# Throwaway matmuls ahead of and between the chain steps of the gated delta section (two-layer hybrid decoder step, one core)

## The reference

```python
def gdn_mixer(h, ...):
    z = h @ w_in                                  # q, k, v, beta, g, gate
    q, k, v = silu(conv(...)), l2-normalized q and k
    o, S = gated_delta_chunked(q, k, v, g, beta, S0)      # chunks of 64 tokens
    return (o * rsqrt(mean(o * o)) * norm_g * silu(zg)) @ w_out

def gated_delta_chunked(...):
    T = inverse(I + A)                            # per chunk, unit triangular
    u, w = T @ (v * beta), T @ (kb * exp(gc))
    def step(S, inp):                             # 4 steps for the sequence of 256
        v_new = u_c - w_c @ S
        o = qg_c @ S + qk_c @ v_new
        S = gl_c * S + kd_c.T @ v_new
        return S, o
```

## Time and profile before

| | |
|---|---|
| median of 3 runs | 1581.13 us (1579.74 to 1581.99) |
| the profiled execution | 1569.06 us, span 1566.9 us |
| mean granted TensorE clock in it | 0.956 |
| PE busy | 1434.2 us (92%) |
| DVE busy | 823.6 us (53%) |
| ACT busy | 628.2 us (40%) |
| POOL busy | 377.8 us (24%) |

### The profile page before, as it was taken

How to read it: one execution, slowest core, us unless ns; L and a number is a source line. 1 busy time by engine, 2 the same in 40 slices (tenths; PEclk the granted TensorE clock), 3 DMA queues, 4 the chain that set the end, 5 groups by cost and what they waited for, 6 DMA issues and landing times.

```text
span 1566.9 us, 30542 instructions
## 1 busy us (share of the span) xinstructions
PE 1434.2 (92%) x12048; PEld 1355.4 (86%) x12048; DVE 823.6 (53%) x1075; ACT 628.2 (40%) x955; POOL 377.8 (24%) x352
## 2 busy tenths in 40 slices
PE   7999999676898799999999999989987778999997
PEld 7999989576588589999989999979876748999996
DVE  4444456974373364444454444478757456544444
ACT  4333346531042353333353333365574234533333
POOL 3333002532131123331113331100017442233200
PEclk9999999898599899999999999999989798999999
DMA  7455532200052145555425555424323014355551
GB/s 279 162 162 185 167 120 95 96 3 33 36 183 79 40 155 162 164 168 186 151 93 163 161 173 183 142 75 148 122 89 123 28 68 148 121 162 166 184 166 49
DMA packets 50616, 203.29 MB, mean 130 GB/s; under 512 B 5697, under 2 KB 5697, under 8 KB 49761
## 3 DMA queue, kind: packets, MB, share of 16 engines
q1 hardware_dynamic: 46224, 181.03, 35.0%
q0 software_dynamic: 4016, 19.81, 3.5%
q10 hardware_dynamic: 288, 1.18, 0.2%
HBM read 192.17 MB, written 9.83 MB: 129 GB/s over the span
## 4 chain that ended last, share of the span: by engine, by line
PE 79%; DVE 11%; ACT 5%; issue 4%; POOL 0%; DMA 0%; DVEq 0%; ACTq 0%; POOLq 0%
PE gemm L2321 21%; PE gemm L2325 21%; PE gemm L2322 21%; DVE wlo L2284 2%; PE gemm L2341 2%; PE job L2354 2%; ACT whi L2279 2%; PE job L689 1%; DVE M L1905 1%; DVE M L2071 1%; PE job L1583 1%; PE job L812 0%; PE job L1657 0%; PE job L720 0%; PE job L1546 0%
## 5 line engine op out<-in xcount | busy, mean ns | idle before, releaser
L2284 DVE TENSOR_TENSOR wlo<-raw,whi 128x1024 fp32r<-128x1024 f32 (+1 forms) x319 | 426.4, 1337 | 461.9 <-ACT whi L2279 461.8
L2321 PE MATMUL gemm<-xhi,whi 128*128 128x288 f32 x2040 | 619.4, 304 | 32.2 <-DVE wlo L2284 22.3
L2325 PE MATMUL gemm<-xlo,whi 128*128 128x288 f32 x2040 | 607.3, 298 | 4.6 <-DVE xlo L395 4.4
L2322 PE MATMUL gemm<-xhi,wlo 128*128 128x288 f32 x2040 | 608.7, 298 | 0.0
L2279 ACT ACTIVATE whi<-raw 128x1024 fp32r<-128x1024 f32 (+1 forms) x319 | 358.1, 1123 | 493.5 <-PE gemm L2325 490.0
L2321 PEld LDWEIGHTS gemm<-xhi,whi 128*128 128x128 f32 x2040 | 389.5, 191 | 43.8 <-DVE wlo L2284 26.0
L2325 PEld LDWEIGHTS gemm<-xlo,whi 128*128 128x128 f32 x2040 | 390.7, 191 | 5.8 <-DVE xlo L395 5.1
L2322 PEld LDWEIGHTS gemm<-xhi,wlo 128*128 128x128 f32 x2040 | 389.9, 191 | 1.4
L2321 PE MATMUL gemm<-hhi,whi 128*128 128x288 f32 x704 | 208.8, 297 | 0.9 <-DVE wlo L2284 0.9
L2322 PE MATMUL gemm<-hhi,wlo 128*128 128x288 f32 x704 | 207.7, 295 | 0.0
L2325 PE MATMUL gemm<-hlo,whi 128*128 128x288 f32 x704 | 207.0, 294 | 0.0
(11 more groups left out here) (381 smaller groups left out, 1299.1 us busy)
## 6 DMA issues: line engine op xcount, KB each, us to landing
raw<-in_w_dram SPq DMA_DIRECT2D x255, 512.0 KB, 3.5
raw<-in_w_dram SPq DMA_DIRECT2D x64, 704.0 KB, 4.0
M<-in_ret_in_dram POOLq DMA_DIRECT2D x1, 2048.0 KB, 9.5
out_ret_s_dram<-M POOLq DMA_DIRECT2D x1, 2048.0 KB, 8.0
s_space<-in_gdn_in_dram POOLq DMA_DIRECT2D x4, 512.0 KB, 7.9
M<-in_gdn_in_dram POOLq DMA_DIRECT2D x4, 512.0 KB, 6.0
out_gdn_s_dram<-s_space POOLq DMA_DIRECT2D x4, 512.0 KB, 4.7
out_gdn_s_dram<-M POOLq DMA_DIRECT2D x4, 512.0 KB, 4.2
```

The lines of the kernel that those rows point to most:

```text
L2284: nc.vector.tensor_tensor(wlo[c % SPL][:, 0:w], raw[c % RAW][:, 0:w], whi[c % SPL][:, 0:w].bitcast(F32), ALU.subtract).then_inc(lo_ready, 1)
L2321: pe.matmul(bank[:, 0:T], whi[s][:, w], hi[:, f0 + q, :], start=first, stop=False)
L2322: pe.matmul(bank[:, 0:T], wlo[s][:, w], hi[:, f0 + q, :], start=False, stop=False)
L2325: mm = pe.matmul(bank[:, 0:T], whi[s][:, w], lo[:, f0 + q, :], start=False, stop=last)
```

## The change

A helper `keep_busy(n)` issues n matmuls on PE whose results nobody reads: `mean` (128 x 128) by the first 256 columns of `xsum`, float32, into `gemm[0]`. Ahead of the chain PE waits until `gemm[0]` was read out for the last time before `gdo`, and issues six. In the chain there are two after each `dKS` (steps 1 to 3), two after `dU` of step 0, two after `dO` of steps 0 to 2, and two after `updates` of steps 1 and 2. With the six that makes 24.

```diff
+            def keep_busy(n):
+                for _ in range(n):
+                    pe.matmul(gemm[0][:, 0:SEQ], C("mean"), xsum[:, 0:SEQ], start=True, stop=True)
+
+            wait_count(pe, bank_free[0], TABLE["gdo"][3][0])
+            keep_busy(6)
             for ck in range(4):
...
                     fin(mm, ("dKS", ck))
+                    keep_busy(2)
...
                 for e in range(2):
                     fin(mms[e], ("dU", ck, e))
+                keep_busy(2 if ck == 0 else 0)
                 if ck == 0:
                     to_channels(0)
...
                 if ck < 3:
                     outputs()
+                    keep_busy(2)
                 if ck in (1, 2):
                     updates(0, ck - 1)
+                    keep_busy(2)
                     if ck == 2:
                         state_products(1)
                     head_norms(ck - 1)
```

## The result

| | before | after |
|---|---|---|
| median | 1581.56 us (4 runs, 1579.74 to 1583.48) | 1562.58 us (4 runs, 1561.32 to 1563.83) |
| ratio | | 0.9894, interval 0.9855 to 0.9932 |
| profiled execution | 1569.06 us, span 1566.9 | 1563.83 us, span 1561.7 |
| PE busy | 1434.2 us | 1443.3 us |

The change saves 19 us by the medians and 5 us by the two profiled executions. The forecast was 7 us, and its range reached down to 1570 us only. In a second comparison the changed kernel again had 1563.5 us and the kernel before 1578.5 us.

The account below looks back on a forecast made before the run. PE, or something it waits for, was taken to bound nearly everywhere, with 24 us at the low clock in the chain. Gains of 7.7 us less 0.3 for overruns, taken as 7.3, gave 1574.0 us, range 1570.0 to 1580.

Parts of the forecast that it names:

- The step that failed: Whole kernel: the profiled execution's gain of 7.3 us applies unchanged to the median, 1581.1 to 1573.8 us, forecast as 1574.0.
- The first rival: Chain: the low-clock stretch is missing in some executions, which then run 1 us slower; median 1578.5 us, chance 0.22.
- `dU` to `dKV` in step 0: Start of the chain: 3.10 us falls to about 2.8, a gain of 0.3, with the pair itself costing 0.6.
- `dKV` to `dKS`: Second term, step 0 into step 1: 4.66 us falls to 3.23, a gain of 1.4, ACT being late next.
- `dKS` to `dU`: Third term, in step 1: 2.86 us falls to 2.6, a gain of 0.3, DVE being late next.
- the overruns: Steps 1 to 3: pairs longer than their pauses cost 0.3 us in all, bounds 0 and 1.2 us.
- The lower bound: Sum of the chain's gains: at worst DVE and ACT hide another 1.4 us and overruns are 1.2, leaving 5.1 us.
- the signs: Profile after: clock 1.00 from 1230 to 1290 us, step 2's `dU` near 1253 instead of 1260.8, `gdo` near 1288.
- The price of the fillers: Matmuls of 256 columns: a pair takes 0.87 us and six 2.6 at the high clock, 1.74 and 5.2 at the low.
- The slower rival: Chain: fillers don't hold the clock, and pairs at 1.74 us on the path add 4.7 us, 1585.8 us; chance 0.09.
- What comes behind: After the chain, `gdo` only shifts; its low-clock loss of 2.7 us may vary by 1.5 us either way.
- The rule on short pauses between groups: Chain: by this rule the clock falls again between groups despite fillers; gain 5.9 us instead of 7.3, 1575.2 us, chance 0.07.

Follow-up runs that it names:

- 2: The kernel before against itself, no edit, with a second profile: 1576.95 us, ratio 0.999 (0.9962 to 1.0017).
- 11: The kernel before, no edit, a single profiled execution: 1578.93 us.
- 12: The kernel before, no edit, another single profiled execution: 1583.48 us.
- narrow control 5: The changed kernel without pairs, its six matmuls ahead of the chain cut from 256 to 16 columns: 1576.6 us, ratio 1.0008 against the kernel before.
- three wide, 6: The changed kernel without pairs and with three matmuls of 256 columns ahead of the chain instead of six: 1569.92 us, ratio 0.9968 against the kernel before.
- pairs alone, 4: The changed kernel without the six matmuls ahead of the chain, pairs kept: 1567.69 us, ratio 0.9935 against the kernel before.
- six alone, 3: The changed kernel without all pairs, the six matmuls ahead of the chain kept: 1563.09 us, ratio 0.9909 against the kernel before.
- after, 1: The changed kernel again, no edit, on one chip with the kernel before: 1563.51 us, ratio 0.9909 (0.9883 to 0.9936).
- lean, 7: The changed kernel without the pairs after `dKS` and after `dU` of step 0: 1561.64 us, ratio 0.9922 against the kernel before.
- experiment 9: The changed kernel without pairs after `dKS` and step 0's `dU`, plus fillers behind the chain and at one place of the first layer's mixer: 1563.22 us, ratio 0.9931.

## Why the prediction was wrong

**The step that failed** is the one that carried a single execution over to the median: "The median of the runs shown is 12 us above that execution; the gain carries over as it is". What was worked out for the profiled execution came out nearly as forecast, 6.7 us in B for 7.3. But its low stretch of 24 us is the short form. The three other profiles of the kernel before (2, 11, 12) have 48, 41 and 48 us, and the narrow control 5 has 41. The gain is not a constant that carries over: it depends on how long the stretch was that the change removes. With A and C nearly constant the time follows B:

| execution | low in the chain, us | B, us |
|---|---|---|
| before, first profile | 24 | 62.1 |
| three wide, 6 | 24 | 62.0 |
| narrow, 5 | 41 | 68.3 |
| before, 11 | 41 | 68.3 |
| before, 2 | 48 | 71.4 |
| before, 12 | 48 | 71.7 |
| pairs alone, 4 | 14 | 60.3 |
| six alone, 3 | 3 | 54.9 |
| after, 1 and first profile | 0 | 55.4 |
| lean, 7 | 0 | 54.7 |

Against the upper group the change saves 68.3 - 55.4 = 13 to 71.7 - 55.4 = 16 us, against the lower one 6.7. 27 of the 40 runs of before in the first two comparisons of the experiments are in the upper group. Weighted so, that makes about 12 us, an estimate from these rows; the second comparison has 13.1 by the means, and 15.0 by the medians, of which that of before lies in the upper group. In the first comparison all four runs of before were in the upper group. The 3 to 6 us that 19 has above B's part come from A, I think, which varied from 1231.8 to 1237.6 us between profiles without any edit there; those runs have no profile, so this is not shown. A holds low stretches of varying length too: in sum over slices of 1 us 95 us in the first profile, 109 in the one after and 116 in 11 and 12. A does not follow their sum closely (1231.8 in experiment 4, with 109 us). The sign was visible: all three runs shown were 11 to 13 us above the profiled execution, and I took that as an offset.

**The first rival had the wrong sign.** I weighed that the low stretch might be missing in some executions. In none of the four profiles of the kernel before was it missing, and in three it was longer; no run of it was under 1568.0 us. The remark beside it, that PE at 83% busy had not raised the clock, pointed at a longer stretch and should have made a rival of its own.

**The terms in the profiled execution.** `dU` to `dKV` in step 0: 2.89 us for 2.8 forecast. `dKV` to `dKS`: 3.13 for 3.23. `dKS` to `dU`: 2.45 for 2.6, and DVE was late next. `dU` to `dKV`: 2.95 for 2.95. `dKV` to `updates`: 3.35 for 3.35. `updates` to head norm: 2.03, the overrun of 0.07. Head norm to `dKS`: 0.96 for 1.05. `dKS` to `dU` of step 2: 2.08 for 2.15. The sum from `dU` to `dU` is 19.84 us instead of 27.75, a gain of 7.9 for 7.7. From there to `gdo` it is 1.2 us more (35.54 for 34.33), which leaves the 6.7 in B; 0.95 of the 1.2 are told below, and the other 0.3 is about what the overruns were put at. The lower bound has a slip: half of the second and third term is 0.85 us and not 1.4. It bore on no end of the range. Of the signs, `dU` of step 2 (1254.43 us) and `gdo` (1289.97) came 1.5 and 2 us later than the places forecast, with A 1.5 us longer, and the clock read 1.00 to 1281 and not to 1290 us.

**The price of the fillers.** A pair was 1.13 us long as a row but moved the next product by 0.97 (1235.61 to 1236.58) for the 0.87 forecast, and by 1.87 at the low clock (1233.71 to 1235.58 in experiment 4) for 1.74. Taking out two kinds of pairs gave 0.7 us in B, nearly all of it between `dU` and `dKV` of step 0 (2.22 instead of 2.89 us), where 0.6 was forecast.

**The slower rival.** The pair at the low clock did stand on the path (experiment 4), but the premise, that full-width fillers don't hold the clock, was wrong for the six: no profile with them shows a low clock in the chain before the end of step 1's updates.

**What comes behind.** The second late updates took 2.09 instead of 1.14 us, since the clock was already low, 0.95 us that my "should only shift" had left out. They took 2.09 us in two profiles of the kernel before as well (2 and 12). C did not change: 271.7.

**The rule on short pauses between groups** (Trainium skill, TensorE: Matmul & The Clock Gate, A second HAM failure mode: psum-queue depth-cycling) says that short idle times between groups of matmuls, in a kernel that cycles through PSUM banks, are frequent enough to make the clock swing. Experiment 3 agrees in step 1, with a fall behind pauses of 1.34 and 0.82 us that was worth 1.6 us, and does not in step 2, where pauses of 1.34 and 0.73 us left the clock at 1.00.

## What to carry to other kernels

A low stretch in a profile can have another length in the next execution of the same program (24, 41 and 48 us here). Take several profiles before pricing it, and look whether the profiled execution lies where the timed runs lie. In this kernel a few full-width throwaway matmuls in the one long pause ahead of the chain were worth more than fillers all along it, and filling half of that pause did not make the gain reliable. Check the pauses for room first: fillers in front of a product that waits for nothing else are paid in full (0.97 us a pair here), and twice that at the low clock.

## What the runs showed of the hardware

- A high busy share did not by itself bring the clock back. In experiment 2 the chain's small products ran at 1.2 GHz from 1240 to 1280 us with PE 78 to 91% busy. With pairs of 128 x 128 by 256 columns among them the low stretch ended after 14 us (experiment 4, one profile).
- The clock fell while PE's rows had no pause: over 411 to 413 us of experiment 9 PE was 100% busy, mostly with products of 32 rows by 512 columns, and the clock fell from 1.00. It had risen behind the fillers about 3 us earlier.
- Six matmuls of 16 columns in 1.41 us gained nothing (ratio 1.0008), and the clock fell 2 us after the start of `dU`; behind six of 256 columns in 2.76 us it stayed at 1.00 there (ratio 0.9909).
- Open: why the clock came back in step 1 in some executions and only in step 2 in others, from the same instructions. The place of the fall does not decide it: in the first profile and in 12 the clock fell 0.7 and 0.8 us ahead of `dU`, and the first low stretch lasted 20.5 us in the one and 48 in the other. Open too: why it fell in the pause in three executions of the kernel before and behind `dU` in 11.
